# Adding eight squared tiles to one block before TensorE sums them, in a three-stage transformer kernel

## The reference

```
x = x + mixer_dilated(rmsnorm(x, attn_norm[0]))        # layer A: 16 heads, three dilations
x = x + conv_ffn(rmsnorm(x, ffn_norm[0]))
x = x + mixer_moba(rmsnorm(x, attn_norm[1]))           # layer B: 16 heads, causal
x = x + conv_ffn(rmsnorm(x, ffn_norm[1]))
h = rms_norm(x, norm1_g)                               # layer C: attention with forget gates,
x = x + mix(attention(h), conv(h), pool(h)) @ w_out    #   a depthwise convolution, a pooling branch
x = x + gated_mlp(rms_norm(x, norm2_g))
```

```
rmsnorm(x, gain) = x * rsqrt(mean(x * x over the 1024 features) + 1e-6) * gain
```

## Time and profile before

| | |
|---|---|
| median of 3 runs | 1072.74 us (1072.71 to 1072.81) |
| the profiled execution | 1073.2 us, span 1071.4 us |
| PE busy | 1060.5 us (99%) |
| DVE busy | 865.4 us (81%) |
| ACT busy | 683.8 us (64%) |
| POOL busy | 342.3 us (32%) |
| granted TensorE clock, mean | 1.000 |

### The profile page before, as it was taken

The page is one execution under the profiler, slowest core; times in us unless marked ns, Lnnn a source line. Parts: engine busy times, 40 slices in busy tenths (PEclk is TensorE's granted clock), DMA queues, the critical chain, the costliest instruction groups (busy, mean ns, idle before and its releaser), DMA issues.

```text
span 1071.4 us, 20926 instructions
## 1 busy us (share of the span) xinstructions
PE 1060.5 (99%) x7404; PEld 978.1 (91%) x7404; DVE 865.4 (81%) x1581; ACT 683.8 (64%) x1256; POOL 342.3 (32%) x368
## 2 busy tenths in 40 slices
PE   8999999999999999999999999999999999999998
PEld 7999999999989999999899899999998998999998
DVE  7666777767799888887776999888896769998886
ACT  6667666666666656566776765555686667665563
POOL 6122212122155333332210555333351005643331
PEclk9999999999999999999999999999999999999999
DMA  8644544446467556535454576555433436665641
GB/s 318 210 144 146 165 146 149 141 142 229 138 201 216 193 194 189 173 103 192 133 177 149 163 215 202 189 186 186 152 116 129 158 119 193 208 203 181 195 157 41
DMA packets 57828, 183.31 MB, mean 171 GB/s; under 512 B 6432, under 2 KB 9760, under 8 KB 57504
## 3 DMA queue, kind: packets, MB, share of 16 engines
q1 hardware_dynamic: 57184, 181.90, 52.9%
q10 hardware_dynamic: 576, 0.52, 0.1%
HBM read 181.35 MB, written 1.05 MB: 170 GB/s over the span
## 4 chain that ended last, share of the span: by engine, by line
PE 93%; DVE 6%; DMA 1%; issue 0%; SPq 0%; ACT 0%; DVEq 0%; ACTq 0%
PE ps L386 23%; PE ps L388 11%; PE ps L562 8%; PE ps L564 8%; PE ps L563 8%; PE ps L1577 6%; PE ps L1579 6%; PE ps L1578 6%; PE ps L1070 2%; PE ps L1071 2%; PE ps L1072 2%; DVE prob L933 1%; DVE w_lo L365 1%; DVE prob L928 1%; PE ps L691 1%; PE ps L735 1%
## 5 line engine op out<-in xcount | busy, mean ns | idle before, releaser
L365 DVE TENSOR_TENSOR w_lo<-w_raw,w_hi 128x1024 fp32r<-128x1024 f32 (+2 forms) x372 | 448.6, 1221 | 50.2 <-ACT w_hi L357 49.6
L357 ACT ACTIVATE w_hi<-w_raw 128x1024 fp32r<-128x1024 f32 (+2 forms) x372 | 356.1, 971 | 162.6 <-PE ps L388 131.0
L386 PE MATMUL ps<-xg,w_hi 128*128 128x512 f32 x1056 | 371.6, 396 | 0.0
L388 PE MATMUL ps<-xg,w_lo 128*128 128x256 f32 x1056 | 293.0, 278 | 0.0
L386 PEld LDWEIGHTS ps<-xg,w_hi 128*128 128x128 f32 x1056 | 198.1, 188 | 44.2
L562 PE MATMUL ps<-w_hi,xg 128*128 128x384 f32 (+1 forms) x576 | 200.7, 349 | 1.5 <-DVE w_lo L365 1.5
L388 PEld LDWEIGHTS ps<-xg,w_lo 128*128 128x128 f32 x1056 | 198.4, 188 | 0.2
L564 PE MATMUL ps<-w_hi,xg 128*128 128x384 f32 (+1 forms) x576 | 193.3, 336 | 0.0
L563 PE MATMUL ps<-w_lo,xg 128*128 128x384 f32 (+1 forms) x576 | 193.0, 335 | 0.0
L1699 POOL TENSOR_TENSOR prob_t<-prob_t,qkT 128x256 f32<-128x256 f32 x63 | 101.2, 1606 | 286.1 <-ACT prob_t L1622 286.1
L1577 PE MATMUL ps<-g_hi,w_hi 128*128 128x256 f32 x528 | 147.9, 280 | 0.0
(11 more groups left out here) (171 smaller groups left out, 1364.7 us busy)
## 6 DMA issues: line engine op xcount, KB each, us to landing
w_raw<-w_stream SPq DMA_DIRECT2D x228, 512.0 KB, 3.7
w_raw<-w_stream SPq DMA_DIRECT2D x140, 384.0 KB, 3.2
w_raw<-w_stream SPq DMA_DIRECT2D x4, 392.0 KB, 3.1
xT<-x_a SPq DMA_DIRECT2D x4, 256.0 KB, 6.3
con<-consts SPq DMA_DIRECT2D x1, 1024.0 KB, 6.4
xT<-x_t SPq DMA_DIRECT2D x4, 256.0 KB, 8.1
conv_taps<-taps SPq DMA_DIRECT2D x1, 1024.0 KB, 6.1
par<-params SPq DMA_DIRECT2D x1, 592.0 KB, 7.5
```

The costliest lines, as they stand in the source:

```text
L357: nc.scalar.activation(w_hi[s][:, 0:w], w_raw[s][:, 0:w], ACT.Copy).then_inc(w_hi_done, 1)
L365: nc.vector.tensor_tensor(w_lo[s][:, 0:w], w_raw[s][:, 0:w], w_hi[s][:, 0:w].bitcast(F32), ALU.subtract).then_inc(w_lo_done, 1)
L386: nc.tensor.matmul(bank(b, 0, 2 * TOK), w_hi[s][:, k * P:(k + 1) * P], xg[:, k, :, :].rearrange("p h t -> p (h t)"), start=(k == 0), stop= ...
L388: last = nc.tensor.matmul(bank(b), w_lo[s][:, k * P:(k + 1) * P], xg_hi[:, k, :], start=False, stop=(k == KT - 1), skip_group_check=True)
```

## The change

GpSimd makes a seventh add, `sqx[0] += sqx[4]`, so that one block holds the sum of all eight. `rows_pe` and `cols_pe` then work on this one block: one row matmul instead of two, two column matmuls instead of four. The counts that are waited for change from 6 to 7 adds a norm (`ADDS`), and all of TensorE's sums now wait for the seventh. At the MLP heads the row matmul leaves `project_first` and stands in step 1, after the third pair of its first chunk. In layer B both column matmuls stand after the fourth chunk.

```
-            if k == KT - 1 and e % 2:
-                rows_pe(eng, e, 0)
-        if e % 2:
-            rows_pe(eng, e, 1)
...
+    ADDS = KT - 1
...
-        for n, (to, other) in enumerate(((0, 1), (2, 3), (0, 2), (4, 5), (6, 7), (4, 6))):
-            if n % 3 < 2:
+        for n, (to, other) in enumerate(((0, 1), (2, 3), (0, 2), (4, 5), (6, 7), (4, 6), (0, 4))):
+            if other in (1, 3, 5, 7):
...
-                eng.wait_ge(x_add, 6 * e + n)
+                eng.wait_ge(x_add, ADDS * e + n)
...
-    def rows_pe(eng, e, h):
-
-        eng.wait_ge(x_add, 6 * e + 3 * h + 3)
-        nc.tensor.matmul(bank(ss_bank(e)), con[:, CON_ONES:CON_ONES + P], sqx[4 * h],
-                         start=(h == 0), stop=(h == 1)).then_inc(x_ss, 1)
...
+    def rows_pe(eng, e):
+
+        eng.wait_ge(x_add, ADDS * (e + 1))
+        nc.tensor.matmul(bank(ss_bank(e)), con[:, CON_ONES:CON_ONES + P], sqx[0], start=True, stop=True).then_inc(x_ss, 1)
+
+    def cols_pe(eng, e):
+
+        eng.wait_ge(x_add, ADDS * (e + 1))
...
-            nc.tensor.matmul(bank(SC, 2 * t, 2), sqx[4 * h][:, t * P:(t + 1) * P], con[:, CON_ONES:CON_ONES + 2],
-                             start=(h == 0 and t == 0), stop=(h == 1), skip_group_check=True).then_inc(c_ss, 1)
+            nc.tensor.matmul(bank(SC, 2 * t, 2), sqx[0][:, t * P:(t + 1) * P], con[:, CON_ONES:CON_ONES + 2],
+                             start=(t == 0), stop=True, skip_group_check=True).then_inc(c_ss, 1)
...
-            if p == 0 and o in (2, 3):
-                cols_pe(eng, 2, o - 2)
+            if p == 0 and o == 3:
+                cols_pe(eng, 2)
...
+                elif i is None and j == 1:
+                    eng.wait_ge(w_lo_done, c + 1)
+                    for k in range(KT):
+                        project2_k(eng, c, 2 * b, k)
+                        if k == 2:
+                            rows_pe(eng, e)
+                    project2(eng, c + 1, 0, None, 2 * b + 1)
```

## The result

| | before | after |
|---|---|---|
| median, both kernels run side by side, 20 runs each | 1072.73 us (1072.27 to 1073.30) | 1074.61 us (1074.09 to 1075.12) |
| the profiled execution | 1073.2 us, span 1071.4 us | 1074.16 us, span 1072.4 us |

The ratio after to before is 1.0017, 95% interval 1.0010 to 1.0024: 1.9 us slower, clear of the noise. Forecast were 1073.0 us, 0.3 slower. The time lies inside the forecast's range of 1070.9 to 1074.7 us, at its upper edge, and the sign was right; but most of the loss was not foreseen.

A forecast was written before the change was run, and what follows sets the result against it. TensorE, busy 1060.5 of 1071.4 us, was taken as the bound. Terms -3.06 (removed matmuls) + 2.58 (head waits) + 0.27 (B) + 0.2 (C) + 0.3 (A) = +0.29 us gave 1073.0 us, range 1070.9 to 1074.7.

The forecast's parts named there:

- The removed matmuls: TensorE in layers A, B, C and the MLP heads: 0.45, 0.45, 0.88 and 1.28 us saved, together 3.06 us.
- allowance of 0.2 for its hand-overs: Layer C: hand-overs following the removed matmuls lose some slack, 0.2 us taken, between 0 and 0.45.
- The seventh add: GpSimd at the first MLP head: kept out by VectorE's second L365, done 0.60 us after it, at 298.59.
- Rival 1: The seventh add is not kept out and takes 0.74 us; change of -2.56 us, 1070.2 us; 12%.
- The waits at the heads: TensorE waits for the seventh add before each MLP row matmul: 0.75, 0.91 and 0.92 us, together 2.58.
- Rival 2: Half the waits at the MLP heads and layer B go: 1.4 us less, 1071.6 us; 15%.
- Layer B: TensorE waits 0.27 us for the seventh add before its columns, bounds 0 and 0.6; 0.45 saved by removed matmuls.
- Layer A: The 0.45 us gained runs into GpSimd's rotation of the first queries: wait of 0.3 us, bounds 0.2 and 1.0.
- After the row matmul: MLP heads: `rms_r` 1.3 us later, `g_lo` for step 2 about 0.3 later, no cost taken; bound 0.6 a head.
- Rival 3: Late `rms_r` makes TensorE wait before the MLPs' first down-projection: 1.8 us more, 1074.8, or 1076.5 us; 12%.
- In TensorE's queue nothing is behind the waiting matmul but projections whose weights are ready: MLP heads, after the row matmul: the projections that follow on TensorE need not wait for weights; no cost taken.
- My own case: The summed forecast, TensorE's queue hiding nothing: +0.29 us, 1073.0 us, reaching from 1072.0 to 1073.9; 61%.

The follow-up runs named there:

- extra_add: Kernel before, with a seventh GpSimd add at the MLP heads that nobody reads; 1072.71 us, ratio 0.9999.
- heads_only: Kernel before, with one block, seven adds and the single row matmul in step 1 at the three MLP heads only; 1075.70 us, ratio 1.0025.
- run 27: Not a run label: the text says two heads "run 27 pairs" of matmuls at 0.347 instead of 0.353 us.
- c_only: Kernel before, with one block, seven adds, one row and two column matmuls in layer C only; 1071.91 us, ratio 0.9989.
- late_row: Changed kernel, with each MLP head's row matmul five pairs later in TensorE's queue; 1072.94 us, ratio 1.0001 against the kernel before.
- reorder: Changed kernel, with its seven adds reordered so that two instead of three follow the last square; 1073.28 us, ratio 1.0008 against the kernel before.
- before_three_waits: Kernel before, with three already satisfied waits put into TensorE's queue in layer A; 1072.89 us, ratio 1.0002.
- abc_only: Kernel before, with one block and seven adds in layers A, B and C only, MLP heads as before; 1071.69 us, ratio 0.9989.
- after_again: The changed kernel, unaltered, profiled a second time; 1074.87 us.
- one_wait: Changed kernel, with one already satisfied wait put into TensorE's queue in layer A; 1074.41 us, ratio 1.0016 against the kernel before.
- reorder_early: Changed kernel, with reordered adds (two after the last square) and the row matmul at the end of step 0; 1073.89 us, ratio 1.0006 against before.
- rows_sooner: Kernel before, six adds kept, with each MLP head's second row matmul two pairs earlier; 1074.22 us, ratio 1.0006.
- rows_sooner_again: Kernel before with each MLP head's second row matmul two pairs earlier, profiled a second time; 1076.48 us.

## Why the prediction came out as it did

**The removed matmuls: right in size.** C gave 0.90 for the forecast 0.88, and needed no allowance of 0.2 for its hand-overs.

**The seventh add: right.** It is shut out for a whole second L365 and ends 0.59 after it (forecast 0.60). Rival 1 (an add of 0.74) is refuted. The page "SBUF — State Buffer" of the Trainium skill, section "Who interferes with whom", states that a VectorE instruction with two SBUF inputs contends with a GpSimd instruction that reads SBUF, and that the one which issues first blocks the other for the whole instruction. The trace agrees with its 0.59. extra_add and heads_only have the same 4.08 to 4.11 us for three adds.

**The waits at the heads: right.** 0.62 + 0.11 = 0.73 us at the first (forecast 0.75). At the second and third the L388 ahead starts at 598.61 and 888.93, so 0.79 and 0.77 of standing, with the restart 0.90 and 0.88 (0.91 and 0.92). Together 2.51 for 2.58. Less the 1.28 of the removed matmuls that makes 1.23, and the heads came out at +0.87. The 0.36 between lie in the cadence: behind the wait the first and second head run 27 pairs at 0.347 instead of 0.353 us, 0.18 less each. The forecast took 0.353 for every pair. Rival 2, half the wait, is refuted.

**Layer B: the size nearly right, the wait wrong.** The stretch gave -0.08 for -0.18. But no 0.27 us is waited for the add; TensorE waits 0.28 for `w_lo` where the first column site stood. Taking a matmul out of a place just ahead of a wait for weights gives nothing, and I had looked only for waits on what the change itself makes.

**Layer A: the wait is there, for another reason.** Forecast 0.3, and 0.95 seen. c_only, with A untouched, has 0.39, after the same long step. Layer A came out at +0.39 and -0.01 in two profiles of one kernel, and at -0.59 in c_only. The first MLP starts at 290.51 to 292.01 us in the seven traces with layer A as before (mean 291.19), and at 290.57 to 291.87 in the seven with it changed (mean 291.14). Whatever A gives can't be read.

**After the row matmul: right as far as it went.** `rms_r` starts 1.01 later (299.60 for 298.59; forecast 1.3), `g_lo` comes 0.38 later against the head's start (0.10 later while the head starts 0.28 sooner; forecast 0.3). Rival 3 did not happen in the changed kernel. In late_row, where the row matmul is later still, the wait for `g_lo` came, at step 3 and with +0.6 in each loop. The forecast's margin of 1.27 us was that of step 2. Step 3 has less, which I had not read: late_row and reorder both wait there.

**The step that failed** is "In TensorE's queue nothing is behind the waiting matmul but projections whose weights are ready", and with it that a head's cost ends with the head. The sum lacks a term: the loops, 1.35 us in the profiled execution. With it goes the silent premise that a pair takes the same time in both kernels. Against the forecast of +0.44 outside layer A, the profile has +1.23: loops +1.35, heads -0.42, layer C -0.22, layer B +0.10. The median of 20 is +1.88. What the 0.65 between is made of is not shown: a third slow loop in most executions (0.65), or the way to the first MLP, which differs by up to 1.5 us between traces. The second profile, with two slow loops, took 1074.87 us, more than the median.

**Luck.** That 1074.61 lies in the range is luck in part. My own case ended at 1073.9; the range went up to 1074.7 for the third rival, which did not happen, and a cost of about the same size stood in its place.

**What the runs show of this term.**

| kernel | TensorE waits for GpSimd in an MLP head | slow loops in the profile | profile less before, from the first MLP on | medians |
|---|---|---|---|---|
| before_three_waits | no | 0 | -0.01 | +0.26 |
| c_only | no | 0 | -0.92 | -1.01 |
| abc_only | no | 0 | -0.99 | -1.23 |
| extra_add | no | 0 | -0.02 | -0.21 |
| late_row | no | 0 | +0.02 | +0.02 |
| reorder | no | 0 | +0.15 | +0.65 |
| after | yes | 2 | +1.23 | +1.88 |
| after_again | yes | 2 | +1.10 | one run |
| one_wait | yes | 2 | +0.97 | +1.78 |
| heads_only | yes | 2 | +2.40 | +2.78 |
| reorder_early | yes | 3 | +1.70 | +0.97 |
| rows_sooner | yes | 3 | +3.02 | +1.30 |
| rows_sooner_again | yes | 3 | +3.50 | one run |

Counting all profiles, 17 of 21 loops behind such a wait are slow, and none of 21 in the kernels without one (the kernel before with its own three, late_row and reorder, whose waits are for VectorE, among these). The heads' own cost in heads_only is 0.87 us and its medians show 2.78, so its unprofiled executions very likely have slow loops too; so with after. Which loops it meets differs between two executions of one kernel. That the changed MLP heads bring the loss about is shown by heads_only, which has it, and abc_only, which does not; extra_add clears the seventh add itself. That it is the wait in them which turns loops slow is likely from this comparison, but not shown. late_row, which takes the wait away, is no clean test: its own wait for `g_lo` turns the third loop fast. And reorder, without a wait for GpSimd, has five executions that are long by the price of two slow loops.

**What stays open.** rows_sooner adds only a wait, and its two profiled executions have three slow loops each, but its other eleven are as short as if they had none. So a wait for GpSimd is not enough to make a loop slow each time; reorder's longer executions suggest that it may not be needed either, and a trace of one of them would tell. In the MLPs of these traces the cadence turns at a wait, at the row matmul or at one of the first two down-projections, from slow to fast and from fast to slow. What decides, I can't say. Nor do the runs show what inside TensorE makes the same instructions take 5.65 and 2.83/2.72 instead of 5.55 and 2.83.

**The better version** is abc_only, 1071.69 us, with one block in A, B and C and the MLP heads as they were: 1.2 us under the kernel before and 2.9 under the changed one. That is 0.1% of the time. c_only has nearly all of it.

## What to carry to other kernels

A matmul taken from a full TensorE gives its time back only where nothing stands close behind it: look at the next wait of each site (here the slack of `w_lo` in layer B, and of `g_lo` at step 3 of the MLPs), not only at the waits that the change adds. Here an operand made by one more GpSimd add beside long VectorE instructions was late by a whole VectorE instruction, so such an add belongs where TensorE comes well after it (layer C), not where it comes within 1 us. And where TensorE's queue is otherwise without a gap, a short wait may cost more than its length: compare the cadence behind it, in the head and in the loop, matmul by matmul, before calling the rest equal.

## What was new of the hardware

- The same sequence of matmuls ran at one of two lasting cadences at a granted clock of 1.00: 16.77 or 16.84 us for two steps, 0.347 or 0.353 for a pair of matmuls, 0.6 to 0.7 us an MLP. It turned from slow to fast at the first down-projection in all three MLPs of the kernel before, and, in two of three heads of the changed one, behind the wait.
- A matmul that follows a wait costs 0.11 us beyond the wait, at all three heads.
- The last step of the rotation on GpSimd took 0.59 to 0.60 us in some traces and 1.18 to 1.36 in others, in kernels with the same code there.
